# Forget gate on eight partitions with a scan, and head norms begun beside earlier products

## What is computed

```python
z = h @ w_in                       # fq, fk, fv, ff, sq, sk, sv, mq, gates
q, k = head_rmsnorm(fq), head_rmsnorm(fk)          # per head of 64
log_f = log_sigmoid(ff + b_forget)                 # 512 tokens x 8 heads
c = cumsum(log_f, axis=tokens)
s = q @ k.T * d**-0.5 + (c[query] - c[key])        # causal, softmax, @ v
```

## Time and profile before

| | us |
|---|---|
| median of 3 runs | 2793.13 (2790.08 to 2794.68) |
| profiled execution | 2801.39, with a span of 2799.6 |
| mean granted clock of TensorE | 0.964 of full |
| busy: TensorE matmul, VectorE, ScalarE, GpSimd | 2585.7, 1674.6, 726.0, 1798.3 |

### The profile page before, as it was taken

The page is one execution under the profiler, slowest core; times in us unless marked ns, Lnnn a source line. Parts: engine busy times, 40 slices in busy tenths (PEclk is TensorE's granted clock), DMA queues, the critical chain, the costliest instruction groups (busy, mean ns, idle before and its releaser), DMA issues.

```text
span 2799.6 us, 36306 instructions
## 1 busy us (share of the span) xinstructions
PE 2585.7 (92%) x12764; PEld 2159.1 (77%) x12764; DVE 1674.6 (60%) x3128; ACT 726.0 (26%) x1296; POOL 1798.3 (64%) x1315
## 2 busy tenths in 40 slices
PE   4989799999899998998889989999999999999998
PEld 2866578888686675677778889999999977777777
DVE  5457531111334224454449998878788388878887
ACT  4158310000222323433311011111112123322332
POOL 2746557676651252375656568998986778777786
PEclk8989899999998998999999999999999999999999
DMA  6224222222210011122123336899997899989897
GB/s 239 90 83 151 91 75 95 101 90 97 104 61 31 31 60 49 46 91 91 63 95 111 119 123 253 310 351 327 350 333 260 317 324 325 329 298 324 314 327 256
DMA packets 160500, 502.83 MB, mean 180 GB/s; under 512 B 12288, under 2 KB 79488, under 8 KB 128896
## 3 DMA queue, kind: packets, MB, share of 16 engines
q1 hardware_dynamic: 96432, 311.98, 31.8%
q0 software_dynamic: 36864, 134.23, 12.9%
q10 hardware_dynamic: 27088, 55.11, 5.2%
HBM read 448.84 MB, written 52.43 MB: 179 GB/s over the span
## 4 chain that ended last, share of the span: by engine, by line
PE 58%; DVE 13%; POOL 10%; DMA 9%; issue 5%; ACT 4%; SPq 0%; ACTq 0%; DVEq 0%; POOLq 0%
PE banks L546 8%; PE banks L548 8%; PE banks L547 8%; POOL W_lo L408 6%; DMA arena<-gates_dram 5%; PE banks L676 3%; PE banks L906 3%; PE banks L907 2%; PE banks L908 2%; PE banks L821 2%; PE banks L823 2%; PE banks L822 2%; PE banks L694 2%; PE banks L652 2%; PE banks L695 2%
## 5 line engine op out<-in xcount | busy, mean ns | idle before, releaser
L408 POOL TENSOR_TENSOR W_lo<-raw,W_hi 128x2048 fp32r<-128x2048 f32 x127 | 586.6, 4619 | 58.8 <-ACT W_hi L1330 53.2
L433 POOL TENSOR_TENSOR W_lo<-raw,W_hi 128x512 fp32r<-128x512 f32 x376 | 493.8, 1324 | 0.0
L436 POOL TENSOR_TENSOR beat<-zero 128x1 f32<-128x1 f32 x94 | 19.3, 205 | 650.8 <-PE banks L696 255.8
L821 PE MATMUL banks<-A_hi,W_hi 128*128 128x384 f32 x1024 | 380.3, 371 | 18.9 <-ACT B_plain L1258 17.9
L823 PE MATMUL banks<-A_hi,W_lo 128*128 128x384 f32 x1024 | 345.3, 337 | 0.0
L822 PE MATMUL banks<-A_lo,W_hi 128*128 128x384 f32 x1024 | 344.3, 336 | 0.0
L906 PE MATMUL banks<-W_hi,B_hi 128*128 128x512 f32 x768 | 306.2, 399 | 33.3 <-DVE B_lo L1839 33.3
L907 PE MATMUL banks<-W_hi,B_lo 128*128 128x512 f32 x768 | 304.6, 397 | 0.0
L908 PE MATMUL banks<-W_lo,B_hi 128*128 128x512 f32 x768 | 304.1, 396 | 0.0
L546 PE MATMUL banks<-A_hi,W_hi 128*128 128x512 f32 x680 | 265.8, 391 | 4.9 <-issue 4.9
L548 PE MATMUL banks<-A_hi,W_lo 128*128 128x512 f32 x680 | 264.7, 389 | 0.0
(11 more groups left out here) (259 smaller groups left out, 5541.6 us busy)
## 6 DMA issues: line engine op xcount, KB each, us to landing
raw<-weights SPq DMA_DIRECT2D x241, 1024.0 KB, 4.9
gelu_dram<-B_plain ACTq DMA_DIRECT2D x64, 384.0 KB
gates_dram<-arena ACTq DMA_DIRECT2D x48, 512.0 KB, 9.1
arena<-gelu_dram SPq DMA_DIRECT2D x64, 384.0 KB, 7.6
arena<-gates_dram SPq DMA_DIRECT2D x64, 384.0 KB, 10.2
W_plain<-weights SPq DMA_DIRECT2D x4, 1024.0 KB, 15.7
X<-x_t SPq DMA_DIRECT2D x1, 2048.0 KB, 14.3
arena<-v_rows,arena POOLq DMA_INDIRECT x128, 8.4
```

Of the source, the lines that this page charges most:

```text
L408: pool.tensor_tensor(W_lo[:, s % 2, :], raw[:, s % 2, :], W_hi[:, s % 2, :].bitcast(F32), ALU.subtract)\
L433: return pool.tensor_tensor(W_lo[:, j, cols], raw[:, j, cols], W_hi[:, j, cols].bitcast(F32), ALU.subtract)
L821: mm(to, lh, rh, start=k == 0, stop=False)
```

## The change

The forget product is turned round: the forget weights are the stationary operand and the tokens move, so that one tile of 8 partitions x 512 tokens comes out, in the fifth place of the branch, behind Qt. VectorE adds the bias and takes -|x| and min(x, 0), ScalarE takes Exp and Ln on 8x512, and VectorE makes the running sum by one `tensor_tensor_scan` behind the head norms. The row of a head is spread over 128 partitions by one plain matmul with a column of the identity, broadcast, as weights. The table `upto` goes, and `b_forget` becomes one column.

The head norms of fox begin beside the Kt tiles, those of swa beside Qt 2. ScalarE waits for its own copy (`lin_free`) before it squares a tile.

The diff, without the tables' and the host's lines:

```diff
...
         merged = at(12288, KD, T)
-        upto = at(16384, 512)
+        c_heads = at(16384, T)[0:HEADS, :]
+        forget, forget_low = at(16896, T)[0:HEADS, :], at(16896 + T, T)[0:HEADS, :]
+        forget_abs, forget_exp, forget_ln = (at(12288 + T * n, T)[0:HEADS, :] for n in range(3))
         ck = at(16896, 2, 512)
         causal = at(17920, P)
-        log_f = at(18048, QT, HEADS)
         swa_nd, swa_mask, swa_bias = at(16384, 256), at(16640, 256), at(16896, 2, 256)
...
                         b = work()
-                        for j in range(QT):
-                            last = mm(bank[4 + b][:, P * j:T], log_f[:, j, h:h + 1].to_broadcast([P, P]),
-                                      upto[:, 0:T - P * j], start=j == 0, stop=j == QT - 1, skip_group_check=True)
-                        last.then_inc(work_ready[b], 1)
+                        mm(bank[4 + b][:, :], ident[0:HEADS, h:h + 1].to_broadcast([HEADS, P]), c_heads,
+                           start=True, stop=True, skip_group_check=True).then_inc(work_ready[b], 1)
                     for p in range(a["parts"]):
...
             for br in BRANCHES:
-                features_on_partitions("A", 2 if br == "swa" else 1)
+                features_on_partitions("A", 1)
                 if br == "fox":
-                    features_on_partitions("A", 2)
-                    tokens_on_partitions("A", 2, QT, beside=head_norm("fox_q", "fox_k"))
-                    for q in range(QT):
-                        b = lin()
-                        lin_done(product(bank[b][:, 0:HEADS], [(act_tile("A", k, P * q, P),
-                                                                (wf_hi[:, k, :], wf_lo[:, k, :]))
-                                                               for k in range(KD)]), b)
+                    b = lin()
+                    lin_done(product(bank[b][0:HEADS, :], [((wf_hi[:, k, :], wf_lo[:, k, :]), act_tile("A", k))
+                                                           for k in range(KD)]), b)
+                    beside = head_norm("fox_q", "fox_k")
+                    features_on_partitions("A", 2, beside=beside)
+                    tokens_on_partitions("A", 2, QT, beside=beside)
                     stage()
                 elif br == "swa":
+                    beside = head_norm("swa_q", "swa_k")
+                    features_on_partitions("A", 1, beside=beside)
                     slot = slab()
...
                                                      for k in range(KD)]), b)
-                    beside = head_norm("swa_q", "swa_k")
+                    next(beside)
                     tokens_on_partitions("A", 1, QT, first=P, width=P, beside=beside)
-                    next(beside)
                 else:
...
 
-            def head_norm(*names):
+            def head_norm(*names, copied=()):
 
...
                         t, n = tiles[i]
+                        if copied:
+                            act.wait_ge(lin_free[copied[i] % 4], copied[i] // 4 + 1)
                         act.activation(S[i % 2][:, 0:n], t, ACT.Square).then_inc(square_ready, 1)
...
                     squares("mem")
+                n0 = at_["tile"]
+                if br == "swa":
+                    beside = head_norm("swa_q", "swa_k", copied=range(n0, n0 + 5))
                 for i in range(4):
...
                         norm("mem")
+                    if br == "swa" and i >= 2:
+                        next(beside)
                     copy_to(Qt[:, i, :])
                 if br == "fox":
+                    skip(1)
+                    take(small_ready)
+                    step(act.activation(forget_exp, forget_abs, ACT.Exp))
+                    act.activation(forget_ln, forget_exp, ACT.Ln, bias=small[0:HEADS, 1:2]).then_inc(small_done, 1)
+                    beside = head_norm("fox_q", "fox_k", copied=[n0 + i for i in range(9) if i != 4])
                     for i in range(4):
+                        next(beside)
                         copy_to(Kt[:, i, :])
-                    beside = head_norm("fox_q", "fox_k")
                     for c in range(2):
                         for q in range(QT):
-                            next(beside)
+                            next(beside, None)
                             copy_to(V[:, q, 256 * c:256 * c + 256], width=256)
-                    next(beside)
-                    skip(QT)
-                    take(small_ready)
-                    step(act.activation(S[1][:, 0:32], S[0][:, 0:32], ACT.Exp))
-                    act.activation(S[2][:, 0:32], S[1][:, 0:32], ACT.Ln, bias=small[:, 1:2]).then_inc(small_done, 1)
                     loaded()
...
                     load(swa_mask, "swa_mask")
+                    next(beside)
                     copy_to(Kt[:, 0, :])
-                    beside = head_norm("swa_q", "swa_k")
                     for q in range(QT):
-                        next(beside)
+                        next(beside, None)
                         copy_to(V[:, q, 0:P], width=P)
...
                 if br == "fox":
+                    n = at_["tile"]
+                    tile(lambda b: dve.tensor_scalar(forget, b[0:HEADS, :], c_("b_forget")[0:HEADS, :], None, ALU.add))
+                    dve.wait_ge(lin_free[n % 4], n // 4 + 1)
+                    dve.scalar_tensor_tensor(out=forget_abs, in0=forget, scalar=-1.0, in1=forget,
+                                             op0=ALU.mult, op1=ALU.min).then_inc(small_ready, 1)
+                    dve.tensor_scalar(forget_low, forget, 0.0, None, ALU.min)
                     head_norm("fox_q", "fox_k")
+                    take(small_done)
+                    dve.tensor_tensor_scan(c_heads, forget_low, forget_ln, 0.0, ALU.add, ALU.subtract)
                     skip(4 + 8)
-                    x = S[3][:, 0:32]
-                    for q in range(QT):
-                        tile(lambda b: dve.tensor_tensor(x[:, HEADS * q:HEADS * q + HEADS], b[:, 0:HEADS],
-                                                         c_("b_forget", 0, 8), ALU.add))
-                    dve.wait_ge(lin_free[(at_["tile"] - 1) % 4], (at_["tile"] - 1) // 4 + 1)
-                    dve.scalar_tensor_tensor(out=S[0][:, 0:32], in0=x, scalar=-1.0, in1=x,
-                                             op0=ALU.mult, op1=ALU.min).then_inc(small_ready, 1)
-                    take(small_done)
-                    dve.scalar_tensor_tensor(out=log_f.rearrange("p q h -> p (q h)"), in0=x, scalar=0.0,
-                                             in1=S[2][:, 0:32], op0=ALU.min, op1=ALU.subtract)
                     stage_end()
```

More of the change, by code:

```diff
@@ L65 @@
         ("g_final", 8), ("g_norm1", 8), ("b_gate", 24), ("g_fox_q", 1), ("g_fox_k", 1), ("g_swa_q", 1),
[L66 removed]
+        ("g_swa_k", 1), ("g_mem", 8), ("g_mem_q", 1), ("g_mem_k", 1), ("g_norm2", 8), ("b_forget", 1),
         ("sinks", 8), ("lambda", 128), ("w_forget", 64), ("w_pool", 128)]
@@ L75 @@
 TABLES = [("ident", 128), ("mean_all", 128), ("mean_64", 128), ("mean_128", 128), ("distance", 896),
-          ("pool_recip", 1024), ("causal", 128), ("upto", 512), ("swa_distance", 256), ("swa_mask", 256), ("iota", 128),
+          ("pool_recip", 1024), ("causal", 128), ("swa_distance", 256), ("swa_mask", 256), ("iota", 128),
           ("iota16", 16)]
@@ L1161, in _ @@
             norm("final")
-            load(upto, "upto")
             load(causal, "causal")
@@ L1955, in _columns @@
         "g_swa_k": twice(i["swa_k_g_2"]), "g_mem": tiles(i["mem_norm_g_2"]), "g_mem_q": tiles(i["mem_q_g_2"]),
-        "g_mem_k": tiles(i["mem_k_g_2"]), "g_norm2": tiles(i["norm2_g_2"]), "b_forget": rows(i["b_forget_2"]),
+        "g_mem_k": tiles(i["mem_k_g_2"]), "g_norm2": tiles(i["norm2_g_2"]), "b_forget": np.concatenate([i["b_forget_2"].reshape(-1), np.zeros(P - HEADS, np.float32)]).reshape(P, 1),
         "sinks": rows(i["swa_sinks_2"]),
@@ L1970, in _tables @@
            "distance": np.abs(p - np.arange(896)[None] + 384),
-           "causal": np.where(np.arange(P)[None] <= p, 0.0, -NEG_INF), "upto": p <= np.arange(512)[None],
+           "causal": np.where(np.arange(P)[None] <= p, 0.0, -NEG_INF),
            "iota": np.broadcast_to(np.arange(P)[None], (P, P)), "iota16": np.broadcast_to(np.arange(16)[None], (P, 16))}
```

1 line of the change is left out of this document (removed).

## The result

The changed kernel takes 2761.99 us (median of four runs, 2760.16 to 2769.69), the kernel before 2793.9 beside it (four runs, 2790.08 to 2794.94): a ratio of 0.9886, with a 95% interval of 0.9871 to 0.9901, or 31.9 us less. The forecast was 2753.0 and its range ended at 2761, so the time lies 1 us outside, on the slow side. The sign and most of the size were right; 8 to 9 us of the forecast gain are missing.

A forecast was written before the change was run, and what follows sets the result against it. TensorE was taken as the main bound, with idle before both attentions and low clock at their starts. Terms summed to -40.1 us: 2761.3 from the profiled execution, 2753.0 for a plain run, range 2748 to 2761.

The forecast's parts named there:

- Step 1: Fox forget product: 96 matmuls replaced by 24 of 512 columns at full clock, 16.96 us to 5.44; -11.5 us.
- The rival of a clock lost over the new product: Only 8 output columns work in the new forget product, so the clock falls; 2760 us, chance 0.08.
- Step 2: Between fox product and attention: gate work beside later tiles, norms and scan covered, idle 1.0 us instead of 4.31; -3.3 us.
- The cover of 0.5 us: Fox gate: square of Qt 0 ready near 806.3 us, TensorE asks for it at 806.9; thin cover, no wait.
- The scan of 1.1 us: VectorE's one 8x512 scan after the fox norms, taken as about 1.1 us and covered by the last value product.
- The drain of 1.38 us: ScalarE table loads: skill's added drain would make TensorE wait 0.8 us, giving -2.5; forecast rejected it on the trace.
- Step 3: Spread of fox head 0: 1280 columns become 512 at full clock, 0.90 us instead of 4.26; -3.4 us.
- 1.0 us should not lower it: Before fox head 0's spread: 1.0 us idle keeps full clock, since 3.37 us idle elsewhere was followed by 1.00.
- Step 4: Spreads of fox heads 1 to 7: each 0.90 us instead of 2.25; -9.4 us.
- the rival of a wait for softmax: Fox attention: spreads come off TensorE but it waits for softmax instead, giving back 9.4 us; 2762 us, chance 0.05.
- Step 5: Swa norms begun earlier: swa attention starts at 1077.8 instead of 1087.82; -10.0 us (bounds -8.5 and -11).
- Step 6: Start of swa attention: idle of 1.7 us instead of 11.47 keeps full clock; -2.5 us (0 to -3.5).

The follow-up runs named there:

- units_only: Changed kernel plus unused full-size matmuls in the first three units of the fox and swa attentions, none in the idle before them; 2762.6 us.
- fill_boundary: Changed kernel plus unused 512-column matmuls in TensorE's idle ahead of the attentions, 3 in fox and 6 in swa; 2759.7 us.
- fill_units: Changed kernel plus unused matmuls in the idle ahead of both attentions (3 fox, 6 swa) and in their first three units (2, 2, 3 and 2, 2, 7); 2757.3 us.
- fill_lean: Changed kernel plus unused matmuls: 6 in the idle before swa, none before fox, and 1, 1, 2 (fox) and 2, 2, 7 (swa) in first units; 2765.9 us.
- spread_twice: Changed kernel with the spread of each head done twice into the same bank; 2776.2 us.

## Why the prediction was wrong by its steps

- **Step 1** (-11.5) held: 24 rows for the forget tile, 5.53 us from 795.85 on in place of 5.44, the clock at 1.00. The rival of a clock lost over the new product fell.
- **Step 2** (-3.3): the sum of both is -13.60 in place of -14.8. The cover of 0.5 us that I called thin was gone: a pass of VectorE that I set at 0.7 took 1.67, and TensorE waited 0.39. The last value product ended 82.3 us after the first fox product, where the prediction's times make it 80.9 (852.6 less 771.7, the start of that product in the profile of before); apart from the wait this is spread over the products in small amounts. The idle behind it was 0.77 in place of 1.0. The norms ended at 850.6 where I had 848.5, and the scan's 1.21 us were still hidden, with 2.5 to spare. The scan of 1.1 us that I took from neighbouring rows was near. The Trainium skill (DVE: opcode table, instruction layouts, handler registers and perf-mode slots, section on feedback) says that the built-in scan runs at half throughput, and the estimate from that, 1.1 us, was near too. The drain of 1.38 us that the Trainium skill (ScalarE: Activation LUTs, What ACT_TABLE_LOAD costs) adds to each load did not show, 1.29 us lying between load and Ln. What steps 1 and 2 do not say is what each part is worth without the other: the 17 us of forget product had been the cover of the late norms. In A the gate alone gave -3.1, the early fox norms alone -1.0, both -13.6.
- **Step 3** (-3.4, came to -0.53) is the first that failed. "1.0 us should not lower it" took the clock as a matter of the idle ahead. The clock held through the idle and the spread, then fell in the narrow matmuls of the first units behind, which I had not looked at: the spread saved 3.2 us and the rest of head 0 lost 2.7. With four extra matmuls over these units the clock stays, and head 0 takes 8.84.
- **Step 4** (-9.4, came to -7.88): the mechanism was right, the price was mis-sized. I divided 2.25 us by the columns; a spread of 512 costs 1.05 rather than 0.90, since 0.19 of it does not go with the columns. Each head is 1.12 shorter in place of 1.35 (2.25 - 1.05 would give 1.20). TensorE stayed without idle, so the rival of a wait for softmax fell.
- **Step 5** (-10.0): the swa attention stands ready 10.1 to 10.2 us sooner, in the change and alone. D shows -8.67 because the clock fell at the fox output product and took 1.5 back. In no step did I ask whether a stretch that kept its clock before would keep it after; I even used that very place as evidence that 3.37 us of idle are harmless.
- **Step 6** (-2.5, came to +0.17) failed with the same premise. The idle did shrink, from 11.47 to 1.52 us, and the clock fell all the same, before the attention began. The step that failed is that 1.7 us, "under the 3.37 that kept 1.00", would keep it: units_only shows it lost behind 1.52 us of idle, and fill_boundary shows that it is lost in the sparse units when the idle is filled.

Sum of the misses: 1.2 + 2.9 + 1.5 + 1.3 + 2.7 = 9.6 us; the clock has nearly all of the 6.9 in steps 3, 5 and 6. The median came out 9.0 above the forecast, which agrees within the scatter of the other stretches. The range was too narrow: its 3 us either way came from the bounds of steps 2, 5 and 6. It had no term for a fall in head 0 or at the output product, nor for two comparisons of the same kernels giving 31.9 and 39.6.

The best of the versions is fill_units: its branches take 4.9 us less than the change's, and its runs 2757.3 us (ratio to before 0.986, interval 0.9843 to 0.9877). Beside the change's 2758.4 in the same comparison that is no measured gain, and fill_lean shows that such a gain can be lost at the next idle.

## What to carry to other kernels

When a long, cheap product is taken away, ask what worked beside it: here its 17 us covered the norms, and removing it alone (with the cheaper spreads) brought 7 us where removing it and starting the norms sooner brought 20.6. That is 30.5 less the 9.9 of the swa norms, a difference and not a run of its own. When summing clock effects, read the clock over the first sparse units behind a boundary, not only the length of the idle, and give each place that holds the clock by a short idle a chance to lose it. Price a lone matmul by two rows of different widths, or by one and a pair, never by its columns alone.

## What the hardware did that I had not expected

- The granted clock went to 0.50 within 5 us after a full product at 1.00, behind an idle of 0.77 us and some 4 us of short matmuls without a wait, and stayed low for about 7 us in fox. In swa it was at 0.50 before an idle of 1.52 us had ended, and stayed there for about 10.
- Behind 3.37 us of idle, with the same 122 us of unbroken work at 1.00 ahead of it, it held in one kernel and fell in another; repeats of one kernel agreed. In all 14 profiles the outcome goes with where the idle lies against the evenly spaced moments at which the clock changes; no run here tried that by itself.
- It fell once in a stretch where TensorE was busy for 100%, behind two 512-column f32 matmuls over 8 partitions in a row (head 5 of spread_twice). Five other heads with the same pair kept it, so the pair alone does not decide.
- These falls reach far: with the fox norms begun early in the kernel before, the swa attention 220 us later took 2.2 us more, with none of its instructions changed.
